# A tenth slot for expert weights in the room of the residual, and expert gathers regrouped, in a two-layer attention, Hyena and mixture-of-experts kernel

## The chip, the cores and the metric

The kernel runs on one core of one Trainium2 chip. The metric is the device time of one execution in microseconds (us), here the median of three runs. A kernel of this kind can be told from another when the two differ by more than about 0.2%, that is 3.6 us.

## The reference

Two layers over 256 latent tokens of width 1024 (with 256 context tokens beside them). Each layer does attention and a Hyena long convolution, then a feed-forward part. In the first layer that part is dense; in the second it is a mixture of eight experts, and it is this part that the change touches:

```
logits = h @ moe_router
top_val, top_idx = top_k(logits, 2); gate = softmax(top_val)
out = 0
for e in range(8):
    out += weight[:, e] * ((silu(h @ w1[e]) * (h @ w3[e])) @ w2[e])
x = x + gate2 * out;  result = rmsnorm(x) * final_g
```

`h` is the normalised and modulated token (1024 wide), `w1` and `w3` are 1024 x 2816 and `w2` is 2816 x 1024, all in float32. Every expert's weights are read once from HBM, whatever the number of tokens that it gets.

## The kernel before, in words

Everything up to the second layer's output projection runs to about 1098 us of the profiled span. Then come a short router stage (to about 1112 us) and the expert stage (to about 1765 us), in which nearly two thirds of all bytes are moved.

**Places.** The experts are worked off in eight places, 0 to 7. Which expert stands at which place is decided on the chip by how many tokens it has; place 0 is always the last expert, so its weights can be asked for before the router has run. A place holds up to 96 tokens in three rounds of 32, but the places in `SHORT` (1, 4 and 7) hold at most 64 and take two rounds. They are called short here, the others (0, 2, 3, 5, 6) long.

**Units.** An expert's weights come in 18 units (`SEQ`, `units_of`): eight of 2 MB for the first two rounds of columns of `w1` and `w3`, four of 1.5 MB for the rest of those columns, five of 2 MB and one of 1 MB for `w2`. The eight places make 144 units, numbered 0 to 143. One list, `SEQ`, gives their order for all engines: in a place "up1" and "up3" of columns 0, the last down part of the place before, "up1" and "up3" of columns 1, down 0, "up1" and "up3" of columns 2, down 1. Place 0 has units 0 to 15 and 20, 21; place 1 has units 16 to 19, 22 to 33 and 38, 39.

**The ring.** A unit is loaded by SP's DMA queue (lines 603 to 623) into a slot of 16 KB a partition (2 MB in all). There are nine (`SLOTS_KB`, `RING`), and unit n takes slot n % 9. SP issues in order; before unit n (from 9 on) it waits until the matmuls of unit n - 9 are done (`e_use`, which PE raises by one after each unit). Units 0 to 5 are issued as soon as the output projection's inputs allow, units 6 and later after its last matmul. PE waits for a unit with `arrived(n)` on the semaphore of its slot.

**The gathers.** Before a place can start, its tokens must be gathered: PE multiplies the token rows `XT` by 0/1 selection matrices and ACT and DVE bring the result, scaled and shifted, to the tile `G` ("gathered", room for three places). `GATHERS` groups the places: place 0 alone, 1 to 3, 4 to 6, and 7. Each gather is cut into `GATHER_STEPS` steps, between which PE uses PSUM banks 6 and 7 in turn. On PE the gather for place e + 1 stands in place e, behind the last of its up matmuls and ahead of down 1 (`gather`, called at lines 2357 and 2358). While it runs no unit is used up.

**What ends it.** The outputs of places 0 to 6 are written to HBM by ACT's queue (`rows_out`); POOL gathers them by token with four indirect DMAs into `token_rows_a` and `token_rows_b` (lines 694 to 698), which lie where the residual `X` was. The residual itself is dead once the router's matmuls (line 2131, semaphore `r_pe`) are done; its tokens live on in `XT`. Place 7 is added by PE straight from PSUM, and the final norm follows.

The later passes, `experts(1)` and `experts(2)`, run only when an expert overflows its room; with these inputs they don't.

Of the kernel before, what the change touches and what calls it, by code (L numbers as in the profile page):

```python
# [14 lines left out]
P = 128  # L15
# [54 lines left out]
KPU = 4  # L70
SLOT = KPU * 4 * BLK
SLOTS_KB = tuple(kb + h for kb in (48, 64, 80, 96, 112, 163, 0, 16, 32) for h in range(0, 16, 4 * KPU))
EARLY_SLOTS = 24 // KPU
RING = len(SLOTS_KB)
SHORT = (1, 4, 7)
LONG_FROM = len(SHORT)
GATHERS = ((0,), (1, 2, 3), (4, 5, 6), (7,))
GATHER_STEPS = (4, 8, 8, 4)
XT_COPIES = 6
GATHER_AT = {es[0]: i_ for i_, es in enumerate(GATHERS)}  # L80
GATHER_OF = {e_: i_ for i_, es in enumerate(GATHERS) for e_ in es}
# [30 lines left out]
N_EXPERT_UNITS = sum(units_of(*q_[1:]) for q_ in SEQ)  # L112


def unit_bases():

    base, n = [{}, {}], 0
    for l in range(2):
        stages = [("u", U_U), ("qkv", QKV_U), ("merge", MERGE_U), ("wo", WO_U)]
        if l == 0:  # L120
            stages += [("up", UP_U), ("down", DOWN_U)]
        for name, count in stages:
            base[l][name] = n
            n += count
    return base, n


def build(nc, t, out):
    base, n_units = unit_bases()
    top = ExitStack()  # L130
    with top:
# [7 lines left out]
        with ExitStack() as instead_of_x:  # L139
            first_row = sb(instead_of_x, "token_rows_a", [P, 2, D])  # L140
            second_row = sb(instead_of_x, "token_rows_b", [P, 2, D])
        with ExitStack() as instead_of_rows:
            sb(instead_of_rows, "gap_summed", [P, 2, D])
            selTs = sb(instead_of_rows, "scatter_rest", [P, NE, L])
# [128 lines left out]
                    sb(here, "gap_" + name, [P, int(kb * 256)])  # L273
                return sb(here, name, shape, dt)

        ering = [at(f"expert_units{n}", kb, [P, SLOT]) for n, kb in enumerate(SLOTS_KB)]
        tri = at("before", 187, [P, P])
        iot = at("iota", 187.5, [P, ROUNDS * CAP])
        logits = at("logits", 191.625, [P, 2, NE])
# [95 lines left out]
        r_cnt = sem("r_cnt")  # L375
        p_sel = sem("p_sel")

        e_in = [sem(f"e_in{n}") for n in range(RING)]
        e_use, e_silu, e_mid, e_t = (sem("e_" + s) for s in ("use", "silu", "mid", "turned"))
        z_d, e_y = sem("z_down"), sem("e_out")  # L380
        y_gated, sc_pe, sc_ev = (sem("scatter_" + s) for s in ("gated", "pe", "ev"))
# [134 lines left out]
        def _(sp):  # L516
# [83 lines left out]
            def experts(g):  # L600
                at_place_of = {0: None}
                for e, kind, r in SEQ:
                    if e not in at_place_of:
                        if e == 1 and g == 0:
                            sp.wait_ge(order_ready, 1)
                        at_place_of[e] = sp.value_load(order_i[0:1, e:e + 1], min_val=0, max_val=NE - 1)
                    who = at_place_of[e]
                    for u in range(units_of(kind, r)):
                        n = unit_at(g, e, kind, r) + u
                        if n >= RING:  # L610
                            sp.wait_ge(e_use, n - RING + 1)
                        elif n == EARLY_SLOTS:
                            sp.wait_ge(lo_done, n_units)
                            sp.wait_ge(unit_done, n_units)
                        ks = len(unit_steps(kind, r, u))
                        if kind == "down":
                            w, at_unit, width = t["moe_w2" if ks == KPU else "moe_w2_rest"], 8 // KPU * r + u if ks == KPU else 0, BLK
                        elif r < 2:
                            w, at_unit, width = t["moe_" + kind], 8 // KPU * r + u, BLK
                        else:  # L620
                            w, at_unit, width = t["moe_" + kind + "_rest"], u, FF_W[2]
                        into, src = ering[n % RING][:, 0:ks * 4 * width], expert_unit(w, who, at_unit)
                        sp.dma_start(into, src).then_inc(e_in[n % RING], 16)
            experts(0)
            sp.wait_ge(flag_ready, 1)
            with sp.If(sp.value_load(overi[0:1, 0:1], min_val=0, max_val=1) == 1):
# [8 lines left out]
        @block.gpsimd  # L635
        def _(pool):
            def load(dst, src, s):
                pool.dma_start(dst, src).then_inc(s, 16)
            load(small[:], t["small"], consts_in)

            def dft_loads():
                load(dftf[:], t["dftf"], dft_in)
                load(dfti[:], t["dfti"], dft_in)

            def square_add(q, k):

                c0 = norm_c0[q]
                pool.wait_ge(n_sq, 8 * q + k + 1)
                if k == 1 and q > 1:
                    pool.wait_ge(n_pe, 8 * q)  # L650
                if k > 1:
                    pool.wait_ge(n_add, adds_before[q] + k - 1)
                one = sq[:, 0, c0:TOK] if k == 1 else square_sum(q)
                nc.gpsimd.tensor_tensor(square_sum(q), one, sq[:, k % 2, c0:TOK], ALU.add).then_inc(n_add, 1)

            def mod_row_loads(first, end):
                for v in range(first, end):
                    if v >= MROW_RING:
                        pool.wait_ge(md_use, v - MROW_RING + 1)
                    load(mring[:, v % MROW_RING, :], t["w_mod_rows"][v], m1_in[v % MROW_RING])  # L660

            for l in range(2):
                if l == 1:
                    load(srows[:], t["cond_rows"], rows_in)
                    load(dftks[1][:], t["dftk"], tap_in[1])
                    for j, v in enumerate(GATE2_ROWS):
                        if j:
                            pool.wait_ge(g2_use, j)
                        load(gate2_unit[:], t["w_mod_rows"][v], g2_in)
                    pool.wait_ge(unit_done, base[0]["down"])  # L670
                    for k, v in enumerate(MROW_LOADS):
                        if k:
                            square_add(2, k)
                        mod_row_loads(v, (*MROW_LOADS, MROWS)[k + 1])
                        if k == 0:
                            load(decays[1], t["decay"], tap_in[1])
                            load(fw3s[1], t["hy_w3"], tap_in[1])
                            for o in range(2):
                                load(fb_rows[1][o], t["hy_bias"][1][:, o], tap_in[1])
                pool.wait_ge(unit_done, base[l]["u"] + 1 - l)  # L680
                dft_loads()

                pool.wait_ge(y_z, (4 if l == 0 else 6))
                pool.wait_ge(y_lo, (2 if l == 0 else 3))
                load(mask[:], t["mask"], bias_in)
                load(bias[:], t["rpb"][l], bias_in)
                for k in range(1, pooled[2 * l + 1]):
                    square_add(2 * l + 1, k)
            pool.wait_ge(unit_done, base[1]["wo"])
            load(tri[:], t["tri"], bias_in)  # L690
            load(iot[:], t["iota"], bias_in)
            pool.wait_ge(g_pe, GATHER_STEPS[0])
            load(final_rows[:], t["final_rows"], final_in)
            pool.wait_ge(row_ready, 1)
            pool.wait_ge(rows_sent, 16 * (NE - 1))
            for j, to in enumerate((first_row, second_row)):
                for c in range(2):
                    pool.indirect_dma_start(to[:, c, :], None, expert_rows,
                                            bass.IndirectOffsetOnAxis(ap=row_i[:, 2 * c + j:2 * c + j + 1], axis=0)).then_inc(row_in[c][j], 16)
# [1048 lines left out]
        def _(pe):  # L1748
# [458 lines left out]
            def experts(g):  # L2207
# [21 lines left out]
                        ins.then_inc(g_pe, 1)  # L2229

                def arrived(n):
                    pe.wait_ge(e_in[n % RING], 16 * (n // RING + 1))

                def up(e, kind, r):
                    n, m = unit_at(g, e, kind, r), ROUNDS * (NE * g + e) + r
# [6 lines left out]
                    at = e - GATHERS[GATHER_OF[e]][0]  # L2242
                    for u in range(units_of(kind, r)):
                        arrived(n + u)
                        W = ering[(n + u) % RING][:, 0:KPU * 4 * w].rearrange("p (k c f) -> p k c f", k=KPU, c=4)
                        for kk, k in enumerate(unit_steps(kind, r, u)):
                            for rr in range(rounds(g, e)):
                                o = part_out(bank, rr, w)
                                for q in range(4):
                                    ins = MM(o[GRP * q:GRP * (q + 1), :], G[:, k, at, GRP * rr:GRP * (rr + 1)], W[:, kk, q, :],  # L2250
                                             start=k == 0 and rr % 2 == 0, stop=k == DK - 1, skip_group_check=True)
                        ins.then_inc(e_use, 1)

                def down(e, r):
# [5 lines left out]
                    for u in range(units_of("down", r)):  # L2260
                        arrived(n + u)
                        if u == 0:
                            pe.wait_ge(e_t, ROUNDS * E + r + 1)
                        W = ering[(n + u) % RING][:].rearrange("p (k c f) -> p k c f", k=KPU, c=4)
                        for kk, k in enumerate(unit_steps("down", r, u)):
                            for rr in range(rounds(g, e)):
                                for q in range(4):
# [5 lines left out]
                def last_down():  # L2273
# [4 lines left out]
                    for u in range(units):  # L2278
                        for rr in range(R):
                            if rr == 0:  # L2280
                                arrived(n + u)
                                if u == 0:
                                    pe.wait_ge(e_t, ROUNDS * (E + 1))
                            W = ering[(n + u) % RING][:].rearrange("p (k c f) -> p k c f", k=KPU, c=4)
                            for kk, k in enumerate(unit_steps("down", 2, u)):
                                for q in range(4):
                                    o, s, c, first = down_part(g, e, rr, q)
# [232 lines left out]
```

## Time and profile before

| | us |
|---|---|
| median of three runs | 1778.02 (1777.67 to 1779.5) |
| the profiled execution's own time | 1778.41 |
| its span, first to last instruction | 1776.6 |
| PE (matmul) busy | 1690.8 |
| DMA: mean over the span | 248 GB/s, 439.79 MB |
| mean granted clock of TensorE | 0.987 |

The profile shows one execution. Its own time is 1.8 us over its span (what lies before the first and after the last instruction) and 0.4 us over the median. PE is the matmul engine, PEld its weight loads, SPq the queue on which SP issues DMAs. The time to landing is counted from the issue of a DMA until its last part has landed; it holds the time that a transfer stands in the queue behind others.

### The profile page before, as it was taken

What the parts mean: (1) busy time and instruction counts of PE and PEld (TensorE: products, weight loads), DVE (VectorE), ACT (ScalarE), POOL (GpSimd) and SP (SyncE); (2) the same over time, 40 slices, a digit from 0 to 9 for tenths busy, and PEclk for the clock granted to TensorE, in tenths of its full rate; (3) what the DMA queues carried; (4) which work ended last, traced back from release to release, by engine and by line L of the source; (5) the groups of instructions that cost most, each with busy time, mean ns of one, the idle gap of its engine ahead of it and who ended that gap; (6) DMA issues with size and microseconds to landing.
All of it is one profiled execution on the core that took longest, in us unless ns stands there. A gap on an engine that the chain in (4) does not pass through costs nothing.

```text
span 1776.6 us, 38526 instructions
## 1 busy us (share of the span) xinstructions
PE 1690.8 (95%) x17640; PEld 1279.5 (72%) x17640; DVE 697.5 (39%) x989; ACT 420.3 (24%) x583; POOL 48.0 (3%) x60
## 2 busy tenths in 40 slices
PE   7999999999899999999999898999999998999986
PEld 3777766788688888886877788775666765776743
DVE  5447656444633333997764563211001010101012
ACT  4233244333422223223533543000000000000001
POOL 0000000002000000220000000000000000000000
PEclk9999999999999999999999998999999999999999
DMA  9731212125223333685322249989999999999995
GB/s 389 300 110 55 100 48 72 60 95 211 105 96 126 127 122 121 247 298 196 119 95 96 99 156 414 343 361 413 427 428 428 428 428 427 428 427 427 428 426 227
DMA packets 46753, 439.79 MB, mean 248 GB/s; under 512 B 5361, under 2 KB 5617, under 8 KB 12418
## 3 DMA queue, kind: packets, MB, share of 16 engines
q1 hardware_dynamic: 40034, 399.47, 56.2%
q0 software_dynamic: 5552, 34.90, 5.3%
q8 instruction: 134, 2.20, 0.5%
q10 hardware_dynamic: 1008, 3.02, 0.4%
q14 instruction: 25, 0.20, 0.0%
HBM read 433.83 MB, written 3.54 MB: 246 GB/s over the span
## 4 chain that ended last, share of the span: by engine, by line
PE 80%; DMA 8%; DVE 7%; ACT 2%; issue 2%; DVEq 0%; SPq 0%; ACTq 0%
PE psum L2250 19%; PE psum L1753 14%; PE psum L1755 13%; PE psum L1754 13%; PE psum L2269 9%; DMA expert_units<-in_moe_up 4%; DMA expert_units<-in_moe_w 2%; PE psum L2227 2%; DMA expert_units<-in_moe_up_rest 1%; ACT units_hi L711 1%; DVE units_lo L1087 1%; PE psum L1992 1%; PE psum L2014 1%; PE psum L1798 1%; DVE squares L1181 1%
## 5 line engine op out<-in xcount | busy, mean ns | idle before, releaser
L2250 PE MATMUL psum<-expert_units,gathered 128*32 128x256 f32 (+1 forms) x8064 | 408.3, 362 | 13.0 <-DMA expert_units<-in_moe_up_rest 6.2
L2250 PEld LDWEIGHTS psum<-expert_units,gathered 128*32 128x32 f32 x8064 | 289.2, 110 | 128.3 <-issue 12.4
L1753 PE MATMUL psum<-h_hi,units_hi 128*128 128x512 f32 (+1 forms) x928 | 344.9, 372 | 13.1 <-DVE h_lo L1169 6.2
L1755 PE MATMUL psum<-h_hi,units_lo 128*128 128x512 f32 (+1 forms) x928 | 336.2, 362 | 0.0
L1754 PE MATMUL psum<-h_lo,units_hi 128*128 128x512 f32 (+1 forms) x928 | 336.1, 362 | 0.0
L1087 DVE TENSOR_TENSOR units_lo<-raw_units,units_hi 128x2048 fp32r<-128x2048 f32 (+2 forms) x88 | 175.2, 1991 | 264.1 <-ACT units_hi L711 264.1
L711 ACT ACTIVATE units_hi<-raw_units 128x2048 fp32r<-128x2048 f32 (+2 forms) x88 | 147.2, 1673 | 415.6 <-PE psum L1755 360.9
L1753 PEld LDWEIGHTS psum<-h_hi,units_hi 128*128 128x128 f32 x928 | 176.6, 190 | 54.7 <-issue 23.0
L2269 PE MATMUL psum<-expert_units,expert_midT 128*32 128x256 f32 x3600 | 201.3, 380 | 12.2 <-DMA expert_units<-in_moe_w 10.0
L1755 PEld LDWEIGHTS psum<-h_hi,units_lo 128*128 128x128 f32 x928 | 176.4, 190 | 27.1
L1754 PEld LDWEIGHTS psum<-h_lo,units_hi 128*128 128x128 f32 x928 | 176.8, 190 | 24.2
L2269 PEld LDWEIGHTS psum<-expert_units,expert_midT 128*32 128x32 f32 x3600 | 124.3, 110 | 84.2 <-DMA expert_units<-in_moe_w 12.1
L1624 DVE TENSOR_TENSOR expert_mid<-expert_silu,psum 128x768 f32<-128x768 f32 (+3 forms) x24 | 19.1, 796 | 358.3 <-PE psum L2250 358.3
L993 ACT ACTIVATE expert_silu<-psum 128x768 f32<-128x768 f32 (+3 forms) x24 | 16.4, 684 | 555.0 <-PE psum L2250 555.0
L1633 DVE STREAM_TRANSPOSE expert_midT<-expert_mid 128x768 f32<-128x768 f32 (+3 forms) x24 | 19.7, 820 | 148.4 <-PE psum L2269 148.1
L1753 PE MATMUL psum<-mid_hi,units_hi 128*128 128x512 f32 x176 | 70.7, 402 | 0.0
L1754 PE MATMUL psum<-mid_lo,units_hi 128*128 128x512 f32 x176 | 69.6, 395 | 0.0
L1755 PE MATMUL psum<-mid_hi,units_lo 128*128 128x512 f32 x176 | 69.6, 395 | 0.0
L1122 DVE SCALAR_TENSOR_TENSOR mod_units<-mod_units,condition_rows 128x1024 f32<-128x1024 f32 x40 | 53.1, 1356 | 1.7 <-DMA mod_units<-in_w_mod_rows 1.6
L1096 DVE TENSOR_TENSOR units_lo<-raw_units,units_hi 128x1024 fp32r<-128x1024 f32 x28 | 34.0, 1224 | 46.3 <-ACT units_hi L721 46.2
L900 ACT ACTIVATE scores<-scores,neg_max 128x512 f32<-128x512 f32 (+1 forms) x48 | 31.3, 652 | 72.4 <-DVE neg_max L1366 72.1
L1753 PE MATMUL psum<-merged_hi,units_hi 128*128 128x512 f32 (+1 forms) x128 | 44.8, 350 | 1.5 <-DVE units_lo L1087 1.5
(326 smaller groups left out, 1689.9 us busy)
## 6 DMA issues: line engine op xcount, KB each, us to landing
expert_units<-in_moe_up SPq DMA_DIRECT2D x64, 2048.0 KB, 30.3
expert_units<-in_moe_w SPq DMA_DIRECT2D x40, 2048.0 KB, 31.4
expert_units<-in_moe_up_rest SPq DMA_DIRECT2D x32, 1536.0 KB, 29.8
raw_units<-in_w_in SPq DMA_DIRECT2D x40, 1024.0 KB, 4.8
raw_units<-in_ffn_w SPq DMA_DIRECT2D x22, 1024.0 KB, 4.9
mod_units<-in_w_mod_rows POOLq DMA_DIRECT2D x20, 1024.0 KB, 6.0
raw_units<-in_ffn_w SPq DMA_DIRECT2D x16, 704.0 KB, 5.6
raw_units<-in_w_pab SPq DMA_DIRECT2D x16, 512.0 KB, 3.6
```

The costliest lines, as they stand in the source:

```text
L711: A(WH[:, s, 0:n], raw[:, s, 0:n], ACT.Copy).then_inc(hi_done, 1)
L900: A(S[:, n % 2, 0:width], S[:, n % 2, 0:width], ACT.Exp, bias=nmax[:, n % 32:n % 32 + 1], accum_out=psums[:, n % 32:n % 32 + 1]).then_inc( ...
L1087: TT(WL[:, s, 0:n], raw[:, s, 0:n], WH[:, s, 0:n].bitcast(F32), ALU.subtract).then_inc(lo_done, 1)
L1096: TT(low, of, high, ALU.subtract).then_inc(lo_done if j else half_lo, 1)
L1122: ins = STT(to, w, 1.0, srows[:, s, :], ALU.mult, ALU.mult, accum_out=mod[:, col, s:s + 1])
L1633: V_.transpose(midT[:, 0:w // GRP, 0:GRP * R].rearrange("p b (r j) -> p r b j", r=R), mid[:, 0:R, 0:w].rearrange("p r (b j) -> p r b j", j ...
L1753: MM(o, wh, xh, start=first, stop=False)
L1754: MM(o, wh, xl, start=False, stop=False)
L1755: return MM(o, wl, xh, start=False, stop=last)
L2227: ins = MM(PS[:, gather_bank(i, j), kk * n * CAP:(kk + 1) * n * CAP], XT[:, c, k * P:(k + 1) * P], sel[:, c, first:first + n, :], start=c ...
L2250: ins = MM(o[GRP * q:GRP * (q + 1), :], G[:, k, at, GRP * rr:GRP * (rr + 1)], W[:, kk, q, :], start=k == 0 and rr % 2 == 0, stop=k == DK - ...
L2269: ins = MM(o, midT[:, k, GRP * s:GRP * (s + 1)], W[:, kk, c, :], start=r + k == 0 and first, stop=r == 2 and k == 5, skip_group_check=True)
```

## The change

The room of the residual becomes a tenth slot, `x_slot`. A table, `slot_table`, gives each unit its slot: ten in turn up to unit 119 (the twelfth use of slot 9, the new one), and after it nine in turn again. `FREED_BY[n]` is the unit whose end frees the slot of unit n: n - 10 while there are ten, n - 9 later. Unit 9, the first in the new slot, waits for the router's last matmul (`r_pe`) and no longer for unit 0. POOL's gathers of rows, which land in the same room, also wait until unit 119 is used up. The gathers become place 0, place 1, places 2 to 4, and places 5 to 7, with 4, 4, 8 and 8 steps: there is no gather in places 3 and 6 any more, one of one place (instead of three) in place 0, and one of three places in place 1 and in place 4.

```diff
@@ -72,10 +72,11 @@
 RING = len(SLOTS_KB)
+X_SLOT, X_SLOT_LAST = RING, 119
 SHORT = (1, 4, 7)
 LONG_FROM = len(SHORT)
-GATHERS = ((0,), (1, 2, 3), (4, 5, 6), (7,))
-GATHER_STEPS = (4, 8, 8, 4)
+GATHERS = ((0,), (1,), (2, 3, 4), (5, 6, 7))
+GATHER_STEPS = (4, 4, 8, 8)
@@ -110,6 +111,24 @@
+def slot_table():
+
+    slot_of, nth_use, freed_by, last = [], [], [], {}
+    slot = -1
+    for n in range(PASSES * N_EXPERT_UNITS):
+        slot = (slot + 1) % (RING + 1)
+        if slot == X_SLOT and n > X_SLOT_LAST:
+            slot = 0
+        slot_of.append(slot)
+        freed_by.append(last.get(slot))
+        nth_use.append(slot_of.count(slot))
+        last[slot] = n
+    return slot_of, nth_use, freed_by
+
+
+SLOT_OF, NTH_USE, FREED_BY = slot_table()
@@ -139,6 +158,8 @@
+        with ExitStack() as behind_router:
+            x_slot = sb(behind_router, "expert_units_x", [P, SLOT])
@@ -273,7 +294,7 @@
-        ering = [at(f"expert_units{n}", kb, [P, SLOT]) for n, kb in enumerate(SLOTS_KB)]
+        ering = [at(f"expert_units{n}", kb, [P, SLOT]) for n, kb in enumerate(SLOTS_KB)] + [x_slot]
@@ -375,7 +396,7 @@
-        e_in = [sem(f"e_in{n}") for n in range(RING)]
+        e_in = [sem(f"e_in{n}") for n in range(RING + 1)]
@@ -607,8 +628,10 @@
-                        if n >= RING:
-                            sp.wait_ge(e_use, n - RING + 1)
+                        if FREED_BY[n] is not None:
+                            sp.wait_ge(e_use, FREED_BY[n] + 1)
+                        elif SLOT_OF[n] == X_SLOT:
+                            sp.wait_ge(r_pe, 1)
@@ -619,8 +642,8 @@
-                        into, src = ering[n % RING][:, 0:ks * 4 * width], expert_unit(w, who, at_unit)
-                        sp.dma_start(into, src).then_inc(e_in[n % RING], 16)
+                        into, src = ering[SLOT_OF[n]][:, 0:ks * 4 * width], expert_unit(w, who, at_unit)
+                        sp.dma_start(into, src).then_inc(e_in[SLOT_OF[n]], 16)
@@ -693,6 +716,7 @@
             pool.wait_ge(rows_sent, 16 * (NE - 1))
+            pool.wait_ge(e_use, X_SLOT_LAST + 1)
@@ -2229,7 +2253,7 @@
-                    pe.wait_ge(e_in[n % RING], 16 * (n // RING + 1))
+                    pe.wait_ge(e_in[SLOT_OF[n]], 16 * NTH_USE[n])
```

Three more lines (before: 2245, 2264, 2284) take the tile of a unit as `ering[SLOT_OF[n + u]]` instead of `ering[(n + u) % RING]`.

## Rows read from the trace of the kernel before

**Rows 1.** Windows of the expert stage: us, busy PE to POOL, PEclk, DMA share, GB/s.
```profile
1069.40:1116.00 46.60, 40.13 (x314) 38.55 (x316) 17.81 (x60) 13.41 (x28) 0.53 (x1) 0.82 1.01 423
1116.00:1220.00 104.00, 104.00 (x1876) 74.77 (x1872) 15.19 (x40) 5.83 (x9) 0.00 (x0) 1.00 0.91 357
1220.00:1440.00 220.00, 218.81 (x4175) 149.33 (x4167) 22.04 (x33) 8.37 (x13) 0.00 (x0) 1.00 1.01 427
1440.00:1700.00 260.00, 253.44 (x4876) 174.56 (x4872) 23.34 (x36) 8.33 (x14) 0.00 (x0) 1.00 1.01 428
1700.00:1757.50 57.50, 40.89 (x788) 26.20 (x784) 9.93 (x12) 2.57 (x4) 3.84 (x4) 1.00 0.91 384
```

**Rows 2.** DMA issues of the expert units: count, KB each, median us to landing.
```profile
expert_units<-in_moe_up SPq DMA_DIRECT2D x64, 2048.0 KB, 30.3
expert_units<-in_moe_w SPq DMA_DIRECT2D x40, 2048.0 KB, 31.4
expert_units<-in_moe_up_rest SPq DMA_DIRECT2D x32, 1536.0 KB, 29.8
expert_units<-in_moe_w_rest SPq DMA_DIRECT2D x8, 1024.0 KB, 31.3
```

**Rows 3.** Timeline of PE (start us, us): places 0 and 1, then place 6.
```profile
1112.71 41.65 PE L2250 MATMUL psum<-expert_units,gathered 128*32 128x256 f32 x768 [0.88 <-issue]
1164.51 15.81 PE L2250 MATMUL psum<-expert_units,gathered 128*32 128x192 f32 x384
1180.25 8.03 PE L2227 MATMUL psum<-select,x_tokens 128*128 128x288 f32 x32
1188.21 10.57 PE L2269 MATMUL psum<-expert_units,expert_midT 128*32 128x256 f32 x192
...
1222.23 14.00 PE L2250 MATMUL psum<-expert_units,gathered 128*32 128x256 f32 x256
...
1649.75 15.95 PE L2250 MATMUL psum<-expert_units,gathered 128*32 128x192 f32 x380
1665.62 4.00 PE L2227 MATMUL psum<-select,x_tokens 128*128 128x96 f32 x32
```

**Rows 4.** Timeline at the end of the router: SP's units 8 and 9, PE.
```profile
1099.03 19.45 SPq L623 DMA_DIRECT2D expert_units<-in_moe_w  x2
1099.57 0.96 PE L2131 MATMUL psum<-router_scaled,x_residual 128*128 128x8 f32 x8
```

**Rows 5.** Issues of units 22, 23 and 24, each with its time to landing.
```profile
L623 SPq DMA_DIRECT2D expert_units<-in_moe_up x1: 342/342/342, 1180.5 to 1180.5; - x1
...
DMA to landing us min/median/max: 10.7/10.7/10.7
...
L623 SPq DMA_DIRECT2D expert_units<-in_moe_up x1: 343/343/343, 1193.8 to 1193.8; - x1
...
DMA to landing us min/median/max: 8.3/8.3/8.3
...
L623 SPq DMA_DIRECT2D expert_units<-in_moe_up x1: 333/333/333, 1198.8 to 1198.8; - x1
...
DMA to landing us min/median/max: 10.3/10.3/10.3
```

**Rows 6.** Busy time and DMA, from unit 22 landed to unit 23 issued.
```profile
1191.30:1193.70 2.40, 2.40 (x52) 1.46 (x48) 0.00 (x0) 0.00 (x0) 0.00 (x0) 1.00 0.00 0
```

**Rows 7.** Time to landing, issues at 1240-1260, 1420-1440, 1500-1520, 1660-1680.
```profile
DMA to landing us min/median/max: 19.6/25.9/30.2
...
DMA to landing us min/median/max: 19.7/19.8/28.2
...
DMA to landing us min/median/max: 36.8/36.8/38.6
...
DMA to landing us min/median/max: 28.6/31.9/33.0
```

**Rows 8.** Timeline of POOL in the last place: the first gather of rows.
```profile
1713.77 1.00 POOL L698 DMA_INDIRECT token_rows_a<-expert_rows,row_index  x1 [601.09 <-DMA expert_rows<-expert_out]
```

More of the change, by code:

```diff
@@ L2244, in up @@
                         arrived(n + u)
-                        W = ering[(n + u) % RING][:, 0:KPU * 4 * w].rearrange("p (k c f) -> p k c f", k=KPU, c=4)
+                        W = ering[SLOT_OF[n + u]][:, 0:KPU * 4 * w].rearrange("p (k c f) -> p k c f", k=KPU, c=4)
                         for kk, k in enumerate(unit_steps(kind, r, u)):
@@ L2263, in down @@
                             pe.wait_ge(e_t, ROUNDS * E + r + 1)
-                        W = ering[(n + u) % RING][:].rearrange("p (k c f) -> p k c f", k=KPU, c=4)
+                        W = ering[SLOT_OF[n + u]][:].rearrange("p (k c f) -> p k c f", k=KPU, c=4)
                         for kk, k in enumerate(unit_steps("down", r, u)):
@@ L2283, in last_down @@
                                     pe.wait_ge(e_t, ROUNDS * (E + 1))
-                            W = ering[(n + u) % RING][:].rearrange("p (k c f) -> p k c f", k=KPU, c=4)
+                            W = ering[SLOT_OF[n + u]][:].rearrange("p (k c f) -> p k c f", k=KPU, c=4)
                             for kk, k in enumerate(unit_steps("down", 2, u)):
```

## The prediction

> **What bounds the kernel now.** I read the windows of the expert stage first, since the change acts only there. From 1220 to 1700 us the DMA engines are busy all the time and move 427 to 428 GB/s; PE is nearly always busy too, but in the last place it stands idle for 57.50 - 40.89 = 16.6 us, waiting for weights [rows 1]. So the end is set by the stream of weights and not by PE. Before 1220 it is the other way: PE is busy for all of 1116 to 1220, and DMA moves 357 GB/s where it could move 428 [rows 1]. That is (428 - 357) / 428 x 104 = 17.3 us of lost DMA time, and whatever of it comes back should shorten the run, as long as DMA has no new gap later.
>
> Why is it lost? The timeline of PE gives the pace. A 2 MB unit of a long place takes 41.65 / 8 = 5.2 us, a 1.5 MB one 15.81 / 4 = 3.95, a 2 MB unit of a short place 14.00 / 4 = 3.5 [rows 3]. The stream needs 2.097 MB / 428 GB/s = 4.90 us for 2 MB, 3.67 for 1.5 MB and 2.45 for 1 MB [rows 1, 2]. A long place has 13, 4 and 1 of them: PE 13 x 5.2 + 4 x 3.95 + 2.6 = 86 us, DMA 80.8 us. A short place takes PE two thirds, 57 us, and DMA 80.8 as before. With full slots DMA is held to PE's pace in place 0; the short places are where DMA falls behind.
>
> The worst hole is at the gather in place 0. SP may issue unit 23 only when PE is through with unit 14, and PE spends 8.03 us on the gather of three places before it starts on unit 14 [rows 3]. Unit 22 is issued at 1180.5 and lands 10.7 us later, at 1191.2; unit 23 follows at 1193.8, and between the two nothing moves, 0 GB/s [rows 5, 6]. Unit 24 comes at 1198.8 [rows 5]. From there the short place 1 frees slots every 3.5 us against 4.9 us of transfer, the queue fills, and times to landing of 19 us and more show that it never runs dry again [rows 7]. **Unit 24 is thus the last one that is late because of its slot**; all later landings follow it at DMA's own pace.
>
> **The tenth slot.** Unit 9 no longer waits for unit 0. SP's two issues of 1099.03 span 19.45 us, so unit 9 went out at about 1118.2; `r_pe` rises after the router's matmuls at 1099.57 + 0.96 = 1100.5 [rows 4]. It goes out 17.6 us earlier, while DMA still has the units before it in hand (423 GB/s up to 1116) [rows 1]. Nobody is behind this wait but unit 10, which waited for the slot of unit 1 and now for that of unit 0. Each later unit is issued one unit of PE's work earlier. For unit 24 this is the end of unit 14 instead of unit 15: 10.57 / 2 = 5.2 us [rows 3].
>
> **The gathers.** A gather of one place takes 4.00 us of PE, one of three takes 8.03 [rows 3]. In place 0 PE is 4.0 us quicker. Unit 24 is then issued at 1180.3 + 4.0 + 5.2 = 1189.5, against 1198.8: 9.3 us earlier. Units 25 and 26 come 5.2 and 3.5 us behind it and find the queue at work, so the full stream starts that much sooner.
>
> Place 1 gets a gather of three that it didn't have (PE +8.03, net 4.0 us later than before), place 3 loses one (net 4.0 earlier), place 4 gets one (4.0 later), place 6 loses one of 4.0 (even). These cost nothing as long as DMA has work queued. The cover is the time to landing: an issue with nothing ahead of it lands in 8.3 us [rows 5]. The queue after the change is longer by one unit (4.9), shorter by DMA's advance (9.3), and shorter or longer by what PE is late or early. After the gather in place 1: 25.9 + 4.9 - 9.3 - 4.0 = 17.5 us; around 1430, where the old gather is gone: 19.8 + 4.9 - 9.3 + 4.0 = 19.4; at the end of place 4: 36.8 + 4.9 - 9.3 - 4.0 = 28; in place 6, with nine slots again from unit 120: 31.9 - 9.3 = 22.6 [rows 7]. All are over 8.3 by 9 us or more. If that cover were gone, each gather would cost its 8 us less what is still queued.
>
> POOL's new wait ends with unit 119, the second unit of 1.5 MB after 1649.75, so at about 1657.7; POOL's first gather of rows goes at 1713.8 [rows 3, 8], 56 us later. It costs nothing, and only those four gathers are behind it.
>
> **Sum.** Slot 5.2, gather 4.0, rest 0: 9.2 us off the end. What follows the last weights (the last down part, the scatter, the norm, the output) is untouched. Where the nearest rows bound it: the slot is worth at least the 4.9 us that a unit streams, less if the queue behind unit 24 was not yet dry, and at most the 5.2. The gather is worth between 0, if unit 24's landing is what counts rather than its issue and something else delays it, and 4.0. Above the sum, the whole deficit of 17.3 us is a ceiling, but most of it is PE's pace in place 0, which neither part touches; 2 us of it could come back through units 25 to 28. The profiled execution took 1778.41 us on its own clock, 0.4 over the median; 1778.0 - 9.2 = **1768.8 us**.
>
> The pace that I take for the stream is the measured one. The Trainium skill has a lower one: "DMA: Bandwidth & Descriptors", section Specifications, puts HBM's limit for one core at about 358 GB/s. By that a 2 MB unit would take an estimated 5.9 us, DMA would be the bound in the long places too, and the slot would be worth 5.9. The trace disagrees with it: 428 GB/s for 480 us on end [rows 1].
>
> **The rivals.**
>
> (a) *Part comes back.* The gather of three, now in place 1, finds a shorter queue than I reckon, because the advance and the gather meet within 60 us of each other. A queue that is 17.5 us on paper and runs out opens a gap before unit 43. That gives back the gather's gain or more: 1778.0 - 5 = 1773.3 us or so. For it speaks that times to landing at 1240 begin at 19.6, not 25.9 [rows 7]; against it, that even 19.6 gives 11.2, over 8.3. 22%.
>
> (b) *Nothing.* A unit counts as landed when its slowest DMA engine is done. If one engine always runs behind, earlier issues only make the others wait for it, and the run stays at 1778. The time from 1191.3 to 1193.7, when no engine moved anything [rows 6], speaks against it: the slowest had caught up as well. PE being the bound at the end would have the same outcome, but it would have to lose the 16.6 us of idle time of the last place first [rows 1]. 10%. The Trainium skill says on the same page, in "Latency and other measured facts", that engines 7 and 15 are usually slower than the rest; no row here names an engine.
>
> (c) *Slower.* Both gathers of three drain the queue. Each stop of 8.03 us and the unit behind it make 13.3 us without an issue, as between units 22 and 23 [rows 5]; with no cover at all 13.3 - 4.9 = 8.4 us are lost in each, 16.8 less 9.2 gained: 1785.6 us. It decides when the time to landing just ahead of the gather falls below about 13 us in both places. I have 17.5 and 28 there. 4%.
>
> **How the numbers follow.** The forecast holds 64%, its own range 1766 to 1770.5. Differences under 0.2% (3.6 us) are what a measurement of this kernel can't tell from none. From the forecast and nearly all of (a) comes "faster", 85%; the rest of (a) and (b) make "same", 11%; (c) 4%. For eight times in ten the range takes in most of (a): 1766.0 to 1773.5.
>
> **What would show it.** Unit 9 issued at about 1100.6; unit 24 at about 1189.5; no stretch of 0 GB/s near 1191; some 394 GB/s in 1116 to 1220 (357 now); 427 or more from there to about 1735; times to landing never under 12 us after 1240; less idle time of PE around 1490 to 1530. If the second gather shows a DMA gap behind it near 1255, (a) holds; if unit 24 is early but the landings of place 4 are not, (b).

## The result, and the profile after

| | before | changed |
|---|---|---|
| median of four runs, us | 1777.85 (1775.06 to 1779.5) | 1767.05 (1764.68 to 1767.95) |
| the profiled execution: span, us | 1776.6 | 1765.5 |
| first expert matmul to the end of the span, us | 663.9 | 654.6 |

The ratio is 0.9939, with a 95% interval of 0.9922 to 0.9956: 10.8 us faster, between 8 and 14. The forecast was 1768.8 us, 9.2 us faster, with a range of 1766.0 to 1773.5.

The third line is used throughout. It is the span less the start of the first expert matmul (1776.6 - 1112.71 and 1765.5 - 1110.93), and I call it **the stage**. It is 9.3 us shorter. The other 1.8 us of the profiled difference lie ahead of the change's first effect on PE, and are no part of its worth: that start wanders (see the end of the experiments).

First the windows of the expert stage of the changed kernel. The last border is moved with the end.

```profile
core 0: us, PE busy (x) PEld busy (x) DVE busy (x) ACT busy (x) POOL busy (x), PEclk, DMA share, GB/s
1069.40:1116.00 46.60, 40.13 (x351) 38.09 (x353) 19.96 (x67) 13.43 (x28) 0.54 (x1) 0.89 1.00 423
1116.00:1220.00 104.00, 104.00 (x1952) 74.80 (x1948) 15.51 (x38) 4.98 (x9) 0.00 (x0) 1.00 0.99 405
1220.00:1440.00 220.00, 219.60 (x4197) 166.05 (x4191) 19.56 (x28) 8.71 (x14) 0.00 (x0) 1.00 1.01 428
1440.00:1690.00 250.00, 249.28 (x4733) 179.69 (x4729) 23.87 (x35) 8.87 (x14) 0.00 (x0) 1.00 1.01 427
1690.00:1747.00 57.00, 45.31 (x817) 31.81 (x806) 9.92 (x12) 2.58 (x4) 3.85 (x4) 0.94 0.91 383
```

Against [rows 1]: DMA moves 405 GB/s in 1116 to 1220, where it moved 357. That is 104 x 48 / 428 = 11.7 us of transfer more in that stretch, of which the earlier start of the stage is a part. Behind it nothing changed, 427 to 428 GB/s. In its last 57 us PE is idle for 11.7 us (16.6 before), so weights still set the end. PE was granted less of its clock there (0.94): a unit at 1719.94 took it 4.42 us, the next of that size 2.81. So part of the smaller idle time is slower work and not less waiting.

The timeline of PE shows the moved gathers:

```profile
1110.93 41.65 PE L2274 MATMUL psum<-expert_units,gathered 128*32 128x256 f32 x768 [0.88 <-issue]
...
1178.47 4.00 PE L2251 MATMUL psum<-select,x_tokens 128*128 128x96 f32 x32
1182.40 10.57 PE L2293 MATMUL psum<-expert_units,expert_midT 128*32 128x256 f32 x192
...
1206.72 1.98 PE L2341 MATMUL psum<-gate_diagonals,ones 128*128 128x512 f32 x4
1208.63 7.98 PE L2293 MATMUL psum<-expert_units,expert_midT 128*32 128x256 f32 x144
...
1248.15 8.03 PE L2251 MATMUL psum<-select,x_tokens 128*128 128x288 f32 x32
...
1485.36 8.03 PE L2251 MATMUL psum<-select,x_tokens 128*128 128x288 f32 x32
```

The gather in place 0 takes 4.00 us in the place of 8.03, and those of three stand at 1248.15 and 1485.36 [rows 3]. The two lines from 1206.72 are 10 us of PE in place 1, the spread of the gates and place 0's last down part of three rounds. Two of the experiments turn on them.

SP's timeline at the start, for units 8, 9, and 10 with 11:

```profile
1098.08 0.43 SPq L646 DMA_DIRECT2D expert_units<-in_moe_w  x1
1099.61 0.33 SPq L646 DMA_DIRECT2D expert_units_x<-in_moe_w  x1
1116.37 5.51 SPq L646 DMA_DIRECT2D expert_units<-in_moe_up_rest  x2
```

Unit 9 goes out at 1099.61, right behind the router's matmuls, where it waited until about 1118 [rows 4].

Next, three issues with their times to landing: unit 24, unit 30 and unit 33.

```profile
L646 SPq DMA_DIRECT2D expert_units<-in_moe_up x1: 333/333/333, 1187.9 to 1187.9; - x1
...
DMA to landing us min/median/max: 9.1/9.1/9.1
...
L646 SPq DMA_DIRECT2D expert_units<-in_moe_up_rest x1: 333/333/333, 1214.1 to 1214.1; - x1
...
DMA to landing us min/median/max: 10.7/10.7/10.7
...
L646 SPq DMA_DIRECT2D expert_units<-in_moe_w x1: 337/337/337, 1223.8 to 1223.8; - x1
...
DMA to landing us min/median/max: 15.0/15.0/15.0
```

Unit 24 is issued at 1187.9, against 1198.8 [rows 5]. From the first expert matmul that is 77.0 us against 86.1. It follows unit 23 (1178.7) by 9.2 us, where before unit 23 followed unit 22 by 13.3.

And the times to landing, for issues in 1260 to 1280, 1420 to 1440, 1480 to 1500 and 1640 to 1660:

```profile
DMA to landing us min/median/max: 20.5/21.9/22.6
...
DMA to landing us min/median/max: 19.3/21.0/23.7
...
DMA to landing us min/median/max: 33.8/37.1/40.4
...
DMA to landing us min/median/max: 26.3/31.3/32.1
```

None comes near to the 8.3 us of an empty queue [rows 5, 7].

One more reading, of the end of the stream. The last expert unit, 143, lands at 1762.0 us before and at 1750.8 in the changed kernel. These are the 20 us ahead of that, before and changed:

```profile
1742.00:1762.00 20.00, 14.87 (x296) 9.34 (x291) 2.33 (x3) 0.00 (x0) 0.00 (x0) 1.00 0.56 237
...
1730.80:1750.80 20.00, 15.71 (x288) 10.58 (x284) 2.42 (x3) 0.00 (x0) 0.00 (x0) 0.93 0.58 244
```

All units were issued by then (the last at 1724.5 and 1711.7), yet only 56 to 58% of the DMA engines' time is used. From about 10 to 3 us ahead of the last landing the share is 0.50 (1752 to 1759) and 0.49 (1741 to 1748). Half of the engines are through with their part some 17 us (an estimate: 42% of 20 us, on half of the engines) before the others. A unit's landing is counted at its last part, so the time to landing tells of the slower engines, and the mean rate of all of them.

### The profile page after: what moved, and what is told of

Same layout as the page of the kernel before. It is cut to its first block, busy times and chain, and to the rows that moved or that the text cites. A ratio compares the mean times of both kernels' runs of the same rounds, so it can differ in the third digit from the quotient of the medians.

```text
span 1765.5 us, 38526 instructions
## 1 busy us (share of the span) xinstructions
PE 1690.8 (96%) x17640; PEld 1305.2 (74%) x17640; DVE 697.5 (40%) x989; ACT 420.7 (24%) x583; POOL 48.2 (3%) x60
## 4 chain that ended last, share of the span: by engine, by line
PE 85%; DVE 7%; DMA 3%; ACT 2%; issue 2%; DVEq 0%; SPq 0%; ACTq 0%
PE psum L2274 22%; PE psum L1777 14%; PE psum L1778 14%; PE psum L1779 14%; PE psum L2293 10%; DMA expert_units<-in_moe_w 2%; PE psum L2251 1%; ACT units_hi L735 1%; DVE units_lo L1111 1%; PE psum L2016 1%; PE psum L2038 1%; PE psum L1822 1%; DVE squares L1205 1%; PE psum L2026 1%; PE psum L1996 1%
## 5 line engine op out<-in xcount | busy, mean ns | idle before, releaser
L2274 PE MATMUL psum<-expert_units,gathered 128*32 128x256 f32 (+1 forms) x7392 | 380.3, 364 | 6.9 <-DMA expert_units<-in_moe_up_rest 5.2
L2274 PEld LDWEIGHTS psum<-expert_units,gathered 128*32 128x32 f32 x7392 | 279.4, 111 | 101.9 <-issue 7.5
L2293 PE MATMUL psum<-expert_units,expert_midT 128*32 128x256 f32 x3280 | 185.5, 379 | 6.8 <-DMA expert_units<-in_moe_w 5.2
L924 ACT ACTIVATE scores<-scores,neg_max 128x512 f32<-128x512 f32 (+1 forms) x48 | 31.3, 652 | 72.4 <-DVE neg_max L1390 72.0
```

Source lines behind the costliest of these rows:

```text
L924: A(S[:, n % 2, 0:width], S[:, n % 2, 0:width], ACT.Exp, bias=nmax[:, n % 32:n % 32 + 1], accum_out=psums[:, n % 32:n % 32 + 1]).then_inc( ...
L2293: ins = MM(o, midT[:, k, GRP * s:GRP * (s + 1)], W[:, kk, c, :], start=r + k == 0 and first, stop=r == 2 and k == 5, skip_group_check=True)
```

## The experiments

Twelve kernels ran. Their ratios have intervals of about 0.0010 to 0.0017 to either side, that is 2 to 3 us. The profile is finer, if the right thing is read in it. I measured two things in each: the stage, and when unit 33 lands, counted from the first expert matmul. Unit 33 ends place 1's second down part; it lands some 50 us behind the gap at the gather of place 0, when the queue is deep again. In the kernel before, its lines are these:

```profile
L623 SPq DMA_DIRECT2D expert_units<-in_moe_w x1: 336/336/336, 1233.0 to 1233.0; - x1
...
DMA to landing us min/median/max: 17.3/17.3/17.3
```

It lands at 1233.0 + 17.3 = 1250.3, which is 137.6 us after the first expert matmul. In the changed kernel it lands at 1223.8 + 15.0 - 1110.9 = 127.9.

| kernel | ratio to before | unit 33 lands | stage |
|---|---|---|---|
| before | 1 | 137.6 | 663.9 |
| before_again | 0.9995 | 137.8 | 664.2 |
| changed | 0.9939 | 127.9 | 654.6 |
| after_again | 0.9941 | 128.2 | 654.5 |
| slot_only | 0.9966 | 132.3 | 658.6 |
| gathers_only | 0.9977 | 132.9 | 660.1 |
| slot_until_9 | 0.9971 | 134.4 | 660.9 |
| slot_until_29 | 0.9941 | 128.3 | 654.7 |
| double_place0 | 0.9960 | 130.6 | 656.8 |
| double_places_1_4 | 0.9974 | 127.0 | 661.5 |
| double_place1 | 0.9948 | 128.4 | 655.2 |
| gather_behind_down | 0.9940 | 128.7 | 656.4 |
| gather_inside_down | 0.9939 | 127.8 | 654.6 |
| inside_and_gates_later | 0.9942 | 126.9 | 653.5 |

In all but one kernel the stage ends 526.2 to 527.7 us after unit 33 has landed. Whatever brings unit 33 forward shortens the run by as much, and whatever doesn't, doesn't. The exception, double_places_1_4, is explained below.

Two more columns tell where DMA loses its time. They are GB/s in the 20 us that begin 76 us after the first expert matmul, where the gap at the gather lies, and in the 12 us that begin at 104, around units 29 to 31. At 428 GB/s nothing is lost; 300 GB/s over 20 us are 6.0 us lost.

| kernel | GB/s from 76 to 96 | us lost | GB/s from 104 to 116 | us lost |
|---|---|---|---|---|
| before | 279 | 7.0 | 420 | 0.2 |
| before_again | 292 | 6.4 | 417 | 0.3 |
| changed | 369 | 2.8 | 428 | 0 |
| after_again | 378 | 2.3 | 424 | 0.1 |
| slot_only | 301 | 5.9 | 410 | 0.5 |
| gathers_only | 371 | 2.7 | 422 | 0.2 |
| double_place0 | 312 | 5.4 | 405 | 0.6 |
| gather_behind_down | 374 | 2.5 | 379 | 1.4 |
| gather_inside_down | 377 | 2.4 | 413 | 0.4 |
| inside_and_gates_later | 388 | 1.9 | 427 | 0 |

**slot_only.** The tenth slot with the old gathers.

```diff
-GATHERS = ((0,), (1,), (2, 3, 4), (5, 6, 7))
-GATHER_STEPS = (4, 4, 8, 8)
+GATHERS = ((0,), (1, 2, 3), (4, 5, 6), (7,))
+GATHER_STEPS = (4, 8, 8, 4)
```

> The tenth slot as in the changed kernel, with the gathers of the kernel before (0; 1 to 3; 4 to 6; 7). Theory (what counts is when unit 24 is issued, and two parts add): unit 24 waits for unit 14 instead of 15, 5.2 us earlier, so 5.2 us under the kernel before and 4 over the changed kernel, about 1772.6. Rival (both parts fill the same hole, each alone gives most of it): 8 us or more under before, about 1769.

Ratio 0.9966 (0.9955 to 0.9978), stage 658.6: 5.5 us under the mean of the two profiles of before (664.05). The slot doesn't fill the gap at the gather. DMA still moves next to nothing for 4 us there:

```profile
1186.00:1190.00 4.00, 4.00 (x80) 2.38 (x76) 0.00 (x0) 0.00 (x0) 0.00 (x0) 1.00 0.14 29
```

In all 5.9 us are lost there, against 6.4 to 7.0 before. What the slot gives is that one unit more is already ahead of the gap when it comes.

**gathers_only.** The kernel before, with the edit above the other way round.

> Nine slots, with the gathers of the changed kernel (0; 1; 2 to 4; 5 to 7). Theory: PE is 4.0 us quicker ahead of unit 14, unit 24 is issued 4.0 us earlier, and the run is 4.0 us under before, about 1773.8. Rival (same hole): 8 us or more under before. Rival (the gathers of three in places 1 and 4 need the tenth slot as cover): less than 2 us under before, with a stretch near 1260 in which DMA moves under 400 GB/s.

Ratio 0.9977 (0.9967 to 0.9988), stage 660.1: 3.9 us under before. DMA moved 428 GB/s in 1220 to 1440, so the nine slots are cover enough. The gap at the gather costs 2.7 us of DMA time, against 6.4 to 7.0: this part does fill it. The two parts give 5.5 + 3.9 = 9.4 us, and both together 9.5 (the mean of the two profiles of the changed kernel is 654.55). They add, and the rival of one shared hole is out.

**slot_until_9.** The tenth slot serves once.

```diff
-X_SLOT, X_SLOT_LAST = RING, 119
+X_SLOT, X_SLOT_LAST = RING, 9
```

> The changed kernel, but the tenth slot is used for unit 9 alone; from unit 19 on each unit waits for the unit nine before it. Theory: unit 24 waits for unit 15 again, 5.2 us later than in the changed kernel, so the run is like gathers_only, about 5 us over the changed kernel. Rival (the slot pays because the stream starts 17.6 us earlier, with unit 9 at 1100): same time as the changed kernel.

Ratio 0.9971 (0.9960 to 0.9982), stage 660.9, where gathers_only has 660.1: 6.4 us over the changed kernel, and about 5 were expected. Unit 9's early start alone is worth nothing: DMA has a longer lead for a while in place 0 and then waits for the same slots.

**slot_until_29.** The same line, with 29.

> The changed kernel, but the tenth slot's last unit is 29; from unit 39 on there are nine slots. Theory (unit 24 to 26 are the last that are late because of a slot; behind them the queue covers everything): the same time as the changed kernel within 1 us; times to landing after 1260 fall from about 20 us to about 15, and DMA still moves 427 GB/s or more. Rival (the slot works as cover for the long places 2 and 3 and the gathers of three): 3 us or more over the changed kernel.

Ratio 0.9941 (0.9929 to 0.9954), stage 654.7, as if the slot were there all the way. The queue is shorter afterwards, by one unit. Times to landing in 1320 to 1380 of this kernel:

```profile
DMA to landing us min/median/max: 14.2/16.8/19.2
```

In the changed kernel the median there was 21.8 us. The slot does its work in three uses, units 9, 19 and 29; from unit 39 on it only lengthens a queue that is long enough. No kernel ran with two uses, so whether the third is needed isn't shown.

**after_again.** The changed kernel once more.

> The changed kernel once more, so that it stands beside the others on one chip. Theory (the parts add): slot_only's and gathers_only's ratios together, 0.9966 x 0.9977 = 0.9943, 9 to 11 us under before. In the profile the first expert matmul should start within 1 us of before's 1112.7 if the 1.8 us by which the changed kernel's profile had it earlier was chance; it starts near 1110.9 again if the change causes it.

Ratio 0.9941 (0.9926 to 0.9956), stage 654.5. The first expert matmul started at 1110.1.

**double_place0.** Each matmul of the gather in place 0 is issued twice; the result is the same.

```diff
-                            for c in range(2):
+                            for c in (0, 1) * (2 if i == 1 else 1):
```

> The changed kernel with every matmul of the gather in place 0 issued twice (the second overwrites the first's result with the same values): 4.0 us more of PE ahead of unit 14. Theory: that is the hole's place, the whole 4.0 us come back, like slot_only. Rival (PE's work has slack in place 0): under 1 us over the changed kernel.

Ratio 0.9960 (0.9946 to 0.9974), stage 656.8, only 2.2 us over the changed kernel. The direction is the theory's, the size is not: 4.0 were expected. One part is that the doubled gather is shorter than twice the single one:

```profile
1178.44 7.39 PE L2251 MATMUL psum<-select,x_tokens 128*128 128x96 f32 x64
```

7.39 us against 4.00, so 3.4 us more. The other is that unit 24, issued 3.3 us later (80.3 after the first expert matmul), finds an emptier queue: it takes 7.8 us to land and not 9.1. Unit 24 so lands 2.0 us later, and not 3.3.

**double_places_1_4.** The same edit with `i in (2, 3)`.

> The changed kernel with every matmul of both gathers of three (in places 1 and 4) issued twice: 16 us more of PE in all. Theory: the queue covers them, PE's idle time at the end shrinks, and the time is that of the changed kernel within 1.5 us; times to landing in places 2 and 3 fall from about 20 to about 12 us. If the cover is thinner than I reckon, a few us come on top, and DMA moves less than 420 GB/s in a stretch between 1260 and 1420. Rival (work of PE counts wherever it is): up to 16 us slower.

Ratio 0.9974 (0.9963 to 0.9986), stage 661.5: 7.0 us over the changed kernel, not within 1.5. Unit 33 lands as early as ever. The windows, a time to landing (1320 to 1380) and PE's waits from 1600 on show why:

```profile
1220.00:1440.00 220.00, 219.47 (x4071) 154.44 (x4067) 18.77 (x27) 8.37 (x13) 0.00 (x0) 1.00 1.00 422
1440.00:1690.00 250.00, 249.43 (x4635) 195.21 (x4628) 23.97 (x35) 8.59 (x13) 0.00 (x0) 1.00 1.00 421
...
DMA to landing us min/median/max: 10.0/12.9/13.6
...
PE psum L2312 <- DVE expert_midT L1657: 5.2, 1, 5.2
PE psum L2274 <- issue: 0.3, 1, 0.3
```

In the changed kernel, PE's waits at the end are for weights:

```profile
PE psum L2274 <- DMA expert_units<-in_moe_up_rest: 5.2, 3, 2.6
PE psum L2293 <- DMA expert_units<-in_moe_w: 5.2, 3, 2.1
```

Here there is none for weights left. PE itself has become the bound: some 16 us more of work were put on an engine that had some 12 us of waits left. The last wait, 5.2 us on DVE, is one more step of the same chain. Place 6 ends later on PE, POOL's gathers of rows start later (1719.6, against 1704.5 in the changed kernel), and DVE has to add those rows before it can multiply the last up part, for which PE then waits:

```profile
1719.62 1.00 POOL L722 DMA_INDIRECT token_rows_a<-expert_rows,row_index  x1 [609.56 <-DMA expert_rows<-expert_out]
...
1748.98 1.29 DVE L1705 SCALAR_TENSOR_TENSOR token_rows_a<-token_rows_b,row_weight,token_rows_a 128x1024 f32<-128x1024 f32 x1 [3.94 <-DMA token_rows_b<-expert_rows,row_index]
1750.30 0.55 DVE L1648 TENSOR_TENSOR expert_mid<-expert_silu,psum 128x384 f32<-128x384 f32 x1
```

The times to landing are down to about 10 to 13 us, and DMA moves 421 to 422 GB/s over these windows. The loss isn't spread evenly:

```profile
1260.00:1370.00 110.00, 110.00 (x2078) 73.46 (x2079) 8.57 (x13) 3.67 (x5) 0.00 (x0) 1.00 1.01 428
1370.00:1390.00 20.00, 20.00 (x376) 14.34 (x372) 4.17 (x6) 0.00 (x0) 0.00 (x0) 1.00 0.96 380
```

The times to landing are 10.0 to 13.9 us in the first of these and 10.0 to 12.1 in the second. So they alone don't tell whether DMA loses time.

**double_place1.** Only the gather in place 1 doubled (`i == 2`).

> The changed kernel with every matmul of the gather in place 1 issued twice, 8.0 us more of PE there and nowhere else. In the run that doubled places 1 and 4, PE waited for no weights at all any more: 16 us more were over the some 12 us of waits for weights that the changed kernel has left. Theory (queue and PE's slack each cover 8): the stage from the first expert matmul to the end stays within 1 us of the changed kernel's 654.6 us. Rival (PE's work costs there as well, the queue of 20 us is no cover): 3 us or more on top, half of what places 1 and 4 gave together.

Ratio 0.9948 (0.9933 to 0.9962), stage 655.2: 0.6 us for 7.8 us more of PE (15.79 us for the doubled gather). The same kind of work costs 2.2 us for 3.4 in place 0. This is the plainest evidence that the gather's place is what counts. DMA fell to 422 GB/s in 1220 to 1440 here too, with times to landing of 9.7 to 15.2 us. That is 3 us of DMA time, and the end moved by only 0.6. The last 20 us before unit 143 lands show where the rest went:

```profile
1732.70:1752.70 20.00, 14.00 (x236) 8.19 (x240) 4.26 (x5) 0.00 (x0) 0.00 (x0) 0.91 0.67 279
```

The share is 0.67 here and 0.58 in the changed kernel, 1.8 us of DMA time in 20: the faster half of the DMA engines is less far ahead. The rows fit this reading: at times to landing near 10 us the faster engines run dry now and then, while the slower ones, which set the end, still have work. The trace names no engine, so it stays a reading.

**gather_behind_down.** An attempt to do better: the gather in place 0 behind both units of the second down part.

```diff
-                    if e + 1 in GATHER_AT:
+                    if e + 1 in GATHER_AT and e:
                         gather(GATHER_AT[e + 1])
                     down(e, 1)
+                    if e == 0:
+                        gather(GATHER_AT[1])
```

> The changed kernel with the gather in place 0 behind the place's second down part (units 14 and 15) instead of ahead of it. Units 24 and 25 are then issued about 4.0 us earlier (1183.6 and 1188.8 for 1187.6 and 1193.0), while unit 26 keeps its time of about 1196.5. Theory (DMA has a hole between the landing of unit 23 and unit 26): 2 to 4 us under the changed kernel, about 0.9925 of before. Rival (the remaining loss is PE's pace, not the order): same as the changed kernel, or up to 1 us over it for the wait on the evictions, which have no down part to hide behind any more.

Ratio 0.9940 (0.9926 to 0.9954), stage 656.4, 1.8 us worse than the changed kernel. PE ahead of the gather and around it, and the issues of units 26 and 30:

```profile
1173.07 4.26 PE L2274 MATMUL psum<-expert_units,gathered 128*32 128x192 f32 x98 [0.85 <-issue]
...
1187.78 4.00 PE L2251 MATMUL psum<-select,x_tokens 128*128 128x96 f32 x32
1192.74 10.57 PE L2274 MATMUL psum<-expert_units,gathered 128*32 128x256 f32 x192 [0.96 <-DVE gathered L1538]
...
L646 SPq DMA_DIRECT2D expert_units<-in_moe_w x1: 333/333/333, 1196.6 to 1196.6; - x1
...
DMA to landing us min/median/max: 8.1/8.1/8.1
...
L646 SPq DMA_DIRECT2D expert_units<-in_moe_up_rest x1: 333/333/333, 1214.1 to 1214.1; - x1
...
DMA to landing us min/median/max: 8.0/8.0/8.0
```

PE stands idle for 0.96 us for the evictions. Units 24 and 25 do land earlier, at 84.7 and 89.6 us instead of 86.1 and 92.6. But the hole didn't close, it moved. The gather now stands between units 15 and 16, so unit 26 is issued 8.7 us behind unit 25, and its 8.1 us to landing are those of a queue as good as empty. In 76 to 96 us 2.5 us are lost, as in the changed kernel (2.3 to 2.8). **A hole follows the gather**, wherever it stands in place 0.

The 1.8 us are lost behind that. Unit 30 waits for unit 20, the first of the down part that stands behind 10 us of PE, and it is issued at 105.9 us after the first expert matmul, where the changed kernel has 103.1. About 1 us of this is the wait for the evictions. Most of the rest lies ahead of the gather: PE paused for 0.85 us at 1172, for nothing that the profile shows, and was 1.7 us late already when unit 22 was issued. Why it paused stays open. DMA lost 1.4 us around unit 30, where the changed kernel lost 0 to 0.1. So this second hole belongs to this kernel; the changed one has next to none.

**gather_inside_down.** The gather between the two units of that down part.

```diff
                         ins.then_inc(e_use, 1)
+                        if u == 0 and between is not None:
+                            gather(between)
...
-                    if e + 1 in GATHER_AT:
+                    if e + 1 in GATHER_AT and e:
                         gather(GATHER_AT[e + 1])
-                    down(e, 1)
+                    down(e, 1, None if e else GATHER_AT[1])
```

> The changed kernel with the gather in place 0 between the two units of the place's second down part: unit 24 is issued 4.0 us earlier than in the changed kernel (73 us after the first expert matmul, not 77), unit 25 as before, and the second of the two units hides the evictions, so PE gets no gap as it did with the gather behind both. Theory (a first hole at unit 24, a second at unit 30, when PE spreads the gates and does the down part of three rounds): unit 25 lands 1.5 to 2 us earlier, unit 30 about 2 us earlier; stage 652.5 to 654. Rival (the second hole eats it all): 654.6.

Ratio 0.9939 (0.9924 to 0.9953), stage 654.6, no gain. The hole moved again, to between units 24 and 25: unit 24 is issued 3.3 us earlier than in the changed kernel, unit 25 0.9 later and 9.3 behind unit 24. 2.4 us are lost in 76 to 96, as much as without the move, and 0.4 around unit 30. Unit 30 lands at 112.4 us instead of 113.9, unit 33 at 127.8 instead of 127.9. The stage is the rival's, 654.6, but not for the rival's reason: a second hole at unit 30 can eat nothing in the changed kernel, where DMA moves 428 and 424 GB/s around it.

**inside_and_gates_later.** As the last, with the gates' matmuls behind the down part.

```diff
-                    if g == 0 and e == 1:
-                        gates_spread()
                     if e:
                         down(e - 1, 2)
+                        if g == 0 and e == 1:
+                            gates_spread()
```

> As gather_inside_down, and the two matmul pairs that spread the gates (2.0 us of PE) behind place 0's last down part instead of ahead of it. Unit 30, which waits for that part's first unit, is issued 2.0 us earlier, at about 101 us after the first expert matmul instead of 103. Theory (two holes): this closes the second one, stage 651.5 to 653, 2 to 3 us under the changed kernel. Rival (DMA's remaining loss is PE's pace in place 0 alone): 654.6.

Ratio 0.9942 (0.9925 to 0.9958), stage 653.5: 1.1 us less than the changed kernel, where 1.6 to 3.1 were expected. The 0.4 us around unit 30 are gone (427 GB/s), and 1.9 us are lost in 76 to 96. It is the shortest stage of all, but its time can't be told from the changed kernel's, and 1.1 us in one profile is little, so no version is claimed to beat that one.

**before_again.** The kernel before, for a second profile.

> The kernel before once more, for a second profile of it. If the stage from the first expert matmul to the end is a steady measure, it is 663.9 us again within 1 us, whatever the start; the start itself was at 1108 to 1116 us in the profiles so far, in kernels that are the same up to there, and may lie anywhere in that.

Ratio 0.9995 (0.9983 to 1.0007), stage 664.2. Its first expert matmul:

```profile
1110.53 24.81 PE L2250 MATMUL psum<-expert_units,gathered 128*32 128x256 f32 x456 [0.88 <-issue]
```

It starts 2.2 us earlier than in the first profile, with no change at all. Over all profiles this start lay between 1108.0 and 1115.7 us.

## Why the prediction was right, point by point

**The bound.** Right. The end follows the stream of weights, and the stage ends 526 to 528 us behind unit 33 in eleven kernels out of twelve and in both profiled first. This says also that the 17.3 us lost ahead of 1220 was the right thing to look at.

**The slot.** 5.2 us were forecast, as one unit of PE's work; 5.5 measured alone. The gain isn't a smaller gap at the gather (5.9 us lost there in slot_only, 6.4 to 7.0 before) but one unit more ahead of it. That unit 9's issue moves by 17 us or more is true and worth nothing, as slot_until_9 shows.

**The gathers.** 4.0 forecast, 3.9 measured alone. Nothing came back in places 1 and 4.

**The sum.** 9.2 forecast, 9.5 in the stage. The timed difference, 10.8 us, is 1.3 us more. It lies within the interval, and the start of the stage wandered by several us between profiles of kernels that are the same up to there; I put the rest down to that, though no run shows it for the timed executions.

**"Unit 24 is the last one that is late because of its slot".** Wrong by one unit, once the tenth slot is there. Before, unit 25 was issued 3.5 us behind unit 24 and landed 4.8 behind it, at DMA's own pace. With ten slots it waits for unit 15, 5.2 us of PE behind unit 14, and lands 6.4 us behind unit 24 in slot_only and 6.6 in the changed kernel (5.7 in its second profile). So in slot_only unit 24 lands 7.1 us earlier than before, but unit 25 only 5.5 earlier and unit 33 5.4. The forecast counted the issue of unit 24 (5.2 earlier) and not its landing, and this is why the sum held: had it gone by the landing of the unit it named, it would have promised 7. That the two came so near is in part luck.

**The cover.** Right in that none was lost, but reckoned too thin: 17.5 us forecast behind place 1's gather, 20.5 to 22.6 found. I had taken the 25.9 us of 1240 to 1260 as the base, which belong to issues ahead of the gather and still growing. The other three were too thin as well: 21.0, 37.1 and 31.3 us found for 19.4, 28 and 22.6. I had taken the whole advance of DMA off the queue each time; but where PE had waited for weights before, its issues move forward with the landings. The measure itself, 8.3 us, was too low: doubled gathers brought the times to landing to 10 to 13 us, and DMA lost 2 us of time in 1370 to 1390 without an empty queue. And PE's idle time around 1490 to 1530 went from 6.5 us (of 1480 to 1540) to none.

**The rivals.** (a) fell: there is no gap behind the gather in place 1. The sum in (a) is 1773.0 and not 1773.3. (b) fell with every run of the table: earlier issues were passed on to the slowest DMA engine as well. But its premise holds, as the last 20 us before unit 143 lands show: about half of the engines run behind the rest. It did no harm at the gather of place 0 because there the slower ones had caught up too, with 0 GB/s in all [rows 6]. (c) fell; what makes the gathers of three expensive once they are doubled is not the queue but PE's own slack, which a forecast of (c) would have had to count.

The Trainium skill's figure that the prediction quoted ("DMA: Bandwidth & Descriptors", Specifications, about 358 GB/s of HBM for one core) is a core's share when both cores of the HBM domain stream. The same page, under "Measured (HBM→SBUF, 128 partitions, SWDGE, issued from GpSimd)", has 425 GB/s for a core alone. This kernel runs on one core, and its trace agrees with the second figure: 427 to 428 GB/s for 470 us on end.

## What to carry to other kernels

A stream that is the bound is late only by the holes in it: find the last stretch in which it has one, and read which engine's work stands between the two issues around it. Extra buffers and work taken away pay up to there, by the amount that the last late transfer comes forward, and nowhere behind it. Work that is only moved within that stretch takes its hole along. A buffer that is used three times at the right moment did what one used twelve times did. Before more is moved under the stream's cover, count the other engine's remaining waits, because those 12 us here were the real limit.

## What the runs showed of the hardware that was not expected

- The DMA engines don't keep step. In the last 20 us before the last expert unit lands, with every unit issued, 56% of their time is used before and 58% in the changed kernel: about half of them finish some 17 us before the others, and the end goes by the slower half.
- The mean rate can fall without an empty queue and almost without a price. In double_place1 it was 422 GB/s in 1220 to 1440, with times to landing of 9.7 to 15.2 us in 1260 to 1420; that is 3 us, and the stage grew by 0.6. Nor is there a clear border: at 10.0 to 13.9 us double_places_1_4 moved 428 GB/s (1260 to 1370), at 10.0 to 12.1 us 380 (1370 to 1390).
- A 2 MB unit lands 7.8 to 8.5 us after its issue when nothing is ahead of it, of which 4.9 us are transfer at the full pace.
- The first expert matmul lay between 1108.0 and 1115.7 us, 0.4% of the span, in profiles of kernels whose PE instructions are the same up to that point. The stage behind it repeated within 0.3 us (663.9 and 664.2; 654.6 and 654.5).
